# Memory tokens requested earlier, diagonal staging shared by two engines, and the loads and staging of a prologue reordered

## What is computed

```python
def reference(x, mem, ...):
    for i in range(2):
        if i == 0:
            proj = rmsnorm(x, e_norm) @ e_w_in
            out_a = gmlp_spatial_gate(gelu(a_u), gelu(a_v), e_gmlp_w, e_gmlp_b)
            out_b = silu(layernorm(causal_depthwise_conv31(a * sigmoid(g), e_conv_w)))
            mix = concatenate([out_a, out_b]) @ e_w_out
        else:
            u = rmsnorm(x, o_norm) @ o_w_in
            y = s5_layer(u, lam, log_dt, b, c, d)      # state 64 per group, 32 groups
            mix = glu(gelu(y) @ o_w_out)
        x = x + mix
        memn = rmsnorm(mem, ca_mem_norm[i])
        x = x + attention(rmsnorm(x), k=memn @ ca_wk[i], v=memn @ ca_wv[i])
        x = x + swiglu(rmsnorm(x))
    return rmsnorm(x)
```

## Time and profile before

| | us |
|---|---|
| median of 2 runs | 5374.97 |
| the two runs | 5334.44 and 5415.51 |
| the profiled execution | 5339.59 |
| span of its slowest core (core 4) | 5338.0 |
| spans of its other cores | 5275.0 to 5325.3 |

### The profile page before, as it was taken

How to read it: one execution, slowest core, us unless ns; L and a number is a source line. 1 busy time by engine, 2 the same in 40 slices (tenths; PEclk the granted TensorE clock), 3 DMA queues, 4 the chain that set the end, 5 groups by cost and what they waited for, 6 DMA issues and landing times.

```text
span 5338.0 us, 96207 instructions; the slowest of 8 cores (5275.0 to 5338.0 us)
## 1 busy us (share of the span) xinstructions
PE 4340.5 (81%) x35399; PEld 3515.4 (66%) x35449; DVE 2148.8 (40%) x4562; ACT 1462.6 (27%) x3458; POOL 298.4 (6%) x320
## 2 busy tenths in 40 slices
PE   0332897989979897888979897988979898888978
PEld 0221587767857687766857586766858577666867
DVE  2354523434343533435342433435252433435252
ACT  0122412243132422233132422233131421333131
POOL 0000000000000000000000000000000000000000
PEclk9866997989889997999889897998889997999889
DMA  4115587765678587665768576665868576675866
GB/s 73 40 58 136 95 137 174 105 134 90 167 127 140 95 139 174 93 133 89 176 125 137 100 114 194 90 138 93 181 120 126 116 108 191 91 141 89 176 120 107
DMA packets 457748, 657.94 MB, mean 123 GB/s; under 512 B 19553, under 2 KB 368433, under 8 KB 446800
## 3 DMA queue, kind: packets, MB, share of 16 engines
q0 software_dynamic: 410560, 427.84, 53.6%
q1 hardware_dynamic: 38480, 223.66, 11.9%
q10 hardware_dynamic: 8256, 0.29, 0.1%
HBM read 1041.95 MB, written 37.62 MB: 202 GB/s over the span
## 4 chain that ended last, share of the span: by engine, by line
PE 67%; DMA 14%; DVE 9%; issue 6%; ACT 4%; ACTq 0%; DVEq 0%; POOL 0%; POOLq 0%; SPq 0%
PE ps L183 65%; DMA ring<-ffn_w_down 5%; DMA ring<-o_w_out 3%; DVE s5t L200 3%; DVE aux L215 3%; PE ps L187 2%; DMA xT<-o_c_re 1%; ACT L197 1%; DMA ring<-ffn_w_gate 1%; DMA xT<-o_c_im 1%; ACT bigbf L197 1%; DVE bigbf L200 1%; DMA ring<-e_w_in 1%; DMA ring<-ffn_w_up 0%; ACT sq L197 0%
## 5 line engine op out<-in xcount | busy, mean ns | idle before, releaser
L183 PE MATMUL ps<-xn,ring 128*128 128x256 bf16 x15488 | 1886.1, 284 | 60.2 <-DVE hbuf L200 31.5
L183 PEld LDWEIGHTS ps<-xn,ring 128*128 128x128 bf16 x15488 | 1562.1, 101 | 380.0 <-issue 147.1
L183 PE MATMUL ps<-bigbf,ring 128*128 128x256 bf16 (+1 forms) x13824 | 1480.5, 278 | 221.8 <-DMA ring<-o_w_out 102.1
L183 PEld LDWEIGHTS ps<-bigbf,ring 128*128 128x128 bf16 x13824 | 1336.1, 109 | 362.4 <-issue 237.4
L197 ACT ACTIVATE scr<-ps 128x256 f32<-128x256 f32 (+1 forms) x992 | 398.5, 405 | 1432.5 <-PE ps L183 1079.0
L200 DVE TENSOR_TENSOR bigbf<-scr,ps 128x256 bf16<-128x256 f32 x704 | 295.7, 421 | 890.1 <-PE ps L183 889.9
L200 DVE TENSOR_TENSOR xT<-xT,ps 128x256 f32<-128x256 f32 x640 | 258.9, 420 | 657.2 <-PE ps L183 639.6
L197 ACT ACT_TABLE_LOAD x204 | 261.7, 1283 | 682.3 <-PE ps L183 349.1
L197 ACT ACTIVATE sq<-xT 128x256 bf16<-128x256 f32 x768 | 259.1, 406 | 370.2 <-DVE xT L200 369.1
L209 DVE SCALAR_TENSOR_TENSOR xn<-xT,gv,rstd 128x256 bf16<-128x256 f32 x768 | 312.5, 479 | 10.4 <-DVE rstd L215 0.5
L197 ACT ACTIVATE bigbf<-ps 128x256 bf16<-128x256 f32 (+1 forms) x544 | 211.3, 396 | 375.1 <-PE ps L183 352.3
(11 more groups left out here) (147 smaller groups left out, 2300.2 us busy)
## 6 DMA issues: line engine op xcount, KB each, us to landing
ring<-scr_s SPq DMA_DIRECT2D x64, 2048.0 KB, 8.5
ring<-ffn_w_gate POOLq DMA_DIRECT2D x80, 1024.0 KB, 10.2
ring<-ffn_w_up POOLq DMA_DIRECT2D x80, 1024.0 KB, 9.1
ring<-ffn_w_down POOLq DMA_DIRECT2D x32, 2112.0 KB, 20.4
ring<-e_w_in POOLq DMA_DIRECT2D x16, 2048.0 KB, 15.9
ring<-ca_wq POOLq DMA_DIRECT2D x16, 2048.0 KB, 19.3
ring<-ca_wo POOLq DMA_DIRECT2D x16, 2048.0 KB, 21.8
ring<-scr_diag SPq DMA_DIRECT2D x16, 1984.0 KB
```

What stands on the lines that cost most here:

```text
L183: self.S.op("pe", lambda h: h.matmul(out, lhsT, rhs, start=start, stop=stop), reads=R, writes=W)
```

## The change

Three edits, all in the prologue.

1. The load of the memory tokens and the first three weight loads of `pro_mem` become a function `pro_mem_loads`, called right after the gains' transpose. `pro_mem` takes the weights from a list.
2. `pro_gmlp_conv` is called right after that, ahead of `pro_s5_loads` and of the loads of `fg` and `bsbc`. Its two temporary tiles lie in `s5t` instead of `bigf`, which now holds the memory tokens.
3. In the staging, every second diagonal is made by ScalarE (an Identity activation with the tap's column as scale) instead of VectorE, with a buffer of its own for the ordering; the DMA of each half waits for both engines.

```diff
--- before.py
+++ after.py
@@ -354,14 +354,17 @@
         pb, bpb = self.bank()
         self.tr(pb[:, 0:128], G, bG, [bpb])
         self.cp(gv[:, 0:G_N], pb[:, 0:G_N], [bpb], cW)
+        need_mem = "ca0" in self.phases or "ca1" in self.phases
+        if need_mem:
+            self.pro_mem_loads()
+        if "l0mix" in self.phases:
+            self.pro_gmlp_conv()
         if "l1mix" in self.phases:
             self.pro_s5_loads()
         self.dma("sp", self.fg[:], p["final_norm"].partition_broadcast(128), [], cW)
         self.dma("sp", self.bsbc[:].rearrange("p g i -> p (g i)"),
                  p["e_gmlp_b"][0].rearrange("g i -> (g i)").partition_broadcast(128), [], cW)
-        if "l0mix" in self.phases:
-            self.pro_gmlp_conv()
-        if "ca0" in self.phases or "ca1" in self.phases:
+        if need_mem:
             self.pro_mem()
         if "l1mix" in self.phases:
             self.pro_s5()
@@ -369,29 +372,33 @@
     def pro_gmlp_conv(self):
         p = self.p
         cW = [self.b_const]
-        wtmp = self.bigf[:, 0, :].rearrange("p (g j) -> p g j", g=4)
-        self.dma("sp", wtmp, p["e_gmlp_w"][0].rearrange("g i j -> i g j"), [], [self.b_bf[0]])
+        wtmp = self.s5t[:, 0, 0:512].rearrange("p (g j) -> p g j", g=4)
+        self.dma("sp", wtmp, p["e_gmlp_w"][0].rearrange("g i j -> i g j"), [], [self.b_s5t[0]])
         for g in range(4):
             pb, bpb = self.bank()
-            self.tr(pb[:, 0:128], wtmp[:, g, :], [self.b_bf[0]], [bpb])
+            self.tr(pb[:, 0:128], wtmp[:, g, :], [self.b_s5t[0]], [bpb])
             self.cp(self.gw[:, g, :], pb[:, 0:128], [bpb], cW)
             self.memset(self.gw[64:128, g, 0:64], 0.0, cW)
-        cw = self.bigf[:, 1, :]
-        self.memset(cw, 0.0, [self.b_bf[1]])
-        self.dma("sp", cw[0:31, :], p["e_conv_w"][0], [], [self.b_bf[1]])
+        cw = self.s5t[:, 1, 0:512]
+        self.memset(cw, 0.0, [self.b_s5t[1]])
+        self.dma("sp", cw[0:31, :], p["e_conv_w"][0], [], [self.b_s5t[1]])
         cwT = self.aux[:, 0, 0:128].rearrange("p (f k) -> p f k", k=32)
         for fc in range(4):
             pb, bpb = self.bank()
-            self.tr(pb[:, 0:128], cw[:, fc * 128:(fc + 1) * 128], [self.b_bf[1]], [bpb])
+            self.tr(pb[:, 0:128], cw[:, fc * 128:(fc + 1) * 128], [self.b_s5t[1]], [bpb])
             self.cp(cwT[:, fc, 0:31], pb[:, 0:31], [bpb], [self.b_aux[0]])
         stage = self.bigbf[:].rearrange("p a b -> p (a b)")
         for half in range(2):
             for i in range(62):
                 fc = half * 2 + i // 31
                 k = i % 31
-                self.ts(stage[:, i * 128:(i + 1) * 128], self.ident[:], cwT[:, fc, k:k + 1], None, ALU.mult, None,
-                        [self.b_aux[0], self.b_const], [self.b_bb[0]])
-            self.dma("sp", self.diag_d[half], stage[:, 0:62 * 128], [self.b_bb[0]], [self.b_diag])
+                if i % 2 == 0:
+                    self.ts(stage[:, i * 128:(i + 1) * 128], self.ident[:], cwT[:, fc, k:k + 1], None, ALU.mult, None,
+                            [self.b_aux[0], self.b_const], [self.b_bb[0]])
+                else:
+                    self.act(stage[:, i * 128:(i + 1) * 128], self.ident[:], AF.Identity, [self.b_aux[0], self.b_const],
+                             [self.b_bb[1]], scale=cwT[:, fc, k:k + 1])
+            self.dma("sp", self.diag_d[half], stage[:, 0:62 * 128], [self.b_bb[0], self.b_bb[1]], [self.b_diag])
 
     def rms_generic(self, src_fn, bsrc, n, gcol, dst_fn, bdst, rstd=None, brstd=None, sqbufs=None):
         if rstd is None:
@@ -414,10 +421,16 @@
             self.stt(dst_fn(dc), src_fn(dc), self.gv[:, gcol + dc:gcol + dc + 1], rstd,
                      ALU.mult, ALU.mult, [bsrc[dc], brstd, self.b_const], [bdst[dc]])
 
+    def pro_mem_loads(self):
+        p = self.p
+        memtok = self.bigf[:, 0:4, :].rearrange("p a b -> p (a b)").rearrange("p (m d) -> p m d", m=2)
+        self.dma("sp", memtok, self.mem_d.rearrange("(m p) d -> p m d", p=128), [], self.b_bf[0:4])
+        self.mem_w = [self.load_w(p["ca_wk"][0], 0, 1024), self.load_w(p["ca_wv"][0], 0, 1024),
+                      self.load_w(p["ca_wk"][1], 0, 1024)]
+
     def pro_mem(self):
         p = self.p
         memtok = self.bigf[:, 0:4, :].rearrange("p a b -> p (a b)").rearrange("p (m d) -> p m d", m=2)
-        self.dma("sp", memtok, self.mem_d.rearrange("(m p) d -> p m d", p=128), [], self.b_bf[0:4])
         memT = self.bigf[:, 4:8, :].rearrange("p a b -> p (a b)").rearrange("p (c m) -> p c m", c=8)
         bmT = [self.b_bf[4 + dc // 2] for dc in range(8)]
         for dc in range(8):
@@ -428,14 +441,14 @@
         for li in range(2):
             self.rms_generic(lambda dc: memT[:, dc, :], bmT, 256, G_MEM + 8 * li,
                              lambda dc: self.xn[:, dc, 0:256], self.b_xn)
-            wk, bwk = self.load_w(p["ca_wk"][li], 0, 1024)
+            wk, bwk = self.mem_w[2 * li]
             for oc in range(8):
                 pb, bpb = self.bank()
                 for dc in range(8):
                     self.mm(pb[:, 0:256], wk[:, dc, oc * 128:(oc + 1) * 128], self.xn[:, dc, 0:256], dc == 0, dc == 7,
                             [bwk, self.b_xn[dc]], [bpb])
                 self.act(self.KT[:, li, oc, :], pb[:, 0:256], AF.Copy, [bpb], [self.b_KT])
-            wv, bwv = self.load_w(p["ca_wv"][li], 0, 1024)
+            wv, bwv = self.mem_w[1] if li == 0 else self.load_w(p["ca_wv"][li], 0, 1024)
             for mc in range(2):
                 for half in range(2):
                     pb, bpb = self.bank()
```

## The result

| | before | after |
|---|---|---|
| ratio of the runs compared | 1 | 1.0113 (95% interval 1.0096 to 1.013) |
| profiled execution, us | 5339.6 | 5390.5 |
| span of its slowest core, us | 5338.0 (core 4) | 5388.9 (core 1) |
| start of the loop, mean of 8 cores, us | 485.0 | 539.3 |
| length of the loop, mean of 8 cores, us | 4819.9 | 4821.0 |

The change makes the kernel 1.1% slower. 5339.6 x 1.0113 is 5400 us, the forecast total. The median of the 11 runs after is 5401.5 us; that of the 10 runs before is 5528 us, because in some executions the cores of a die are slowed whatever the kernel, in seven of these ten, and among them the 5415.5 us that went into the 5375 us shown ahead of the prediction; the ratio is made without them, from runs of 5334.4 to 5341.3 us before and 5385.9 to 5404.6 us after.

A forecast was written before the change was run, and what follows sets the result against it. It took 64 small transfers on ScalarE's queue to end the prologue. Staging end 106.4, loads 8, 27.2 and 1, transfers 90, company 3 give squares at 236 us, 60 later: 5400 us in total, range 5362 to 5462.

The forecast's parts named there:

- What bounds the prologue: Prologue: 64 small transfers on ScalarE's queue set its end; tokens and staging are ready 23 us before ScalarE is.
- Part 1 and 2: Prologue: earlier calls of the weight loads and an earlier request of the memory tokens gain 0 us each.
- Part 3, the staging: Staging of the diagonals: starts at 73 us, ends at 106.4 instead of 141, 35 us earlier but worth 0.
- the startup is relieved: Rival, 11%: with 4-byte packets gone from the startup, gains chain faster and staging starts 19 us sooner; +41, 5381 us.
- Part 4, what the reordering moves: ScalarE's stream: small and xT loads wait behind the staging until 106.4 us, so squares start at 236, 60 us later.
- the sum of the small loads: Behind the staging: o_lam loads 8 us together, two o_log_dt 27.2, first xT landing 1 us later; bounds 16 to 67.
- The 63 transfers: Rest of the xT loads on ScalarE's queue: 1.43 us each, 90 us together, bounds 86 and 110.
- The sum against the shown median: Whole kernel: 5400 us is 0.5% more than the shown median of 5375, 1.1% more than the profiled execution.
- Cheap small loads: Rival, 20%: behind the staging the four small loads land in 4.1 us each, 16 and not 35; +41 us, 5380.
- dear ones: Rival, 8%: o_lam_im keeps its 35.3 us and the diagonals' write delays the rest, 31 us on top; 5431 us.
- a change that counts as intended: Rival, 1%: the change does what it says and counts, which needs tokens or staging to be last in the prologue.
- The loop's rhythm: Rival, 5%: in the loop, the later start gives core 4 the pace of core 1, 53 us less, 5347 us.

The follow-up runs named there:

- e6: The kernel before, with a buffer of its own for each of the 64 loads to xT, so none waits for the one before; fastest run 5314.5 us.
- e7: The changed kernel, with the three early weight loads called in pro_mem again; one run, 5398.8 us.
- e2: The changed kernel, with the call of the S5 loads moved back and the staging on VectorE alone; ratio 1.0002 against the kernel before.
- e1: The changed kernel, with the call of the S5 loads moved back and the staging still split; ratio 1.0076 against the kernel before.
- e3: The changed kernel, with the staging on VectorE alone and the S5 loads' call left behind it; ratio 1.0118 against the kernel before.
- e4: The changed kernel, with only the four small loads issued ahead of memory loads and staging again; ratio 1.0103 against the kernel before.
- e8: The changed kernel, with the 64 transfers first and unchained, small loads unchained behind the staging, fg and bsbc in own buffers; fastest run 5284.6 us.
- e9: The kernel of e8, with the four small loads issued by SyncE instead of ScalarE; ratio 0.9916 against the kernel before.

## Why the prediction was right, and where it was not

**What bounds the prologue: right.** That the 64 small transfers on ScalarE's queue, and neither the tokens nor the staging, set the end of the prologue is shown by e6: unchaining them alone starts the loop 15 us sooner, and on cores 2 to 5 the squares 22 us sooner, close to the 23 of the prediction.

**Part 1 and 2: right.** The weights moved by nothing (e7), the early tokens were worth about 1 us (e2).

**Part 3, the staging: the end right to 4 us, by errors that cancel.** It started at 63.5 us, not 73. The rival "the startup is relieved" was real, at under a third of its 19 us: the last gain was issued 5.5 us sooner. And `e_gmlp_w`, which I had given 9 us, 4 of them behind the tokens, took 5.3: it landed beside the tokens (50.7 us against 49.8), with no `o_log_dt` ahead of it. But a half took 16.9 and 15.3 us on ScalarE, not 14 and 12.7. The term that was mis-sized is the 0.30 us for the 128 x 128 form, which I placed between the 254 and 403 ns of rows 6: it takes 403 ns, as long as 128 x 256, and 0.49 us from one to the next.

**Part 4, what the reordering moves: right in mechanism; the sum of the small loads right by luck.** From the end of the staging to the landing of the first transfer I had 39 us (8 + 27.2 + 1, and 3 for company); on core 1 it took 36 (102.3 to 138.5). Its terms were off both ways: `o_lam_re` and `o_lam_im` took 13.4 and 13.7 us to land, not 4.1 each, but the next issues did not wait for these landings, so they cost the 1.5 us of their issues and not 8; the two `o_log_dt` took 22.7 and 11.6 us (17.2 is their median), 34 and not 27.2. The 63 transfers, 90 us forecast, took 93 (138.5 to 231.4), 1.47 us each. The 2.0 us of the Trainium skill's page ("DMA: Bandwidth & Descriptors", section "Anatomy of one DMA — SWDGE (gpsimd) path") would have given, as an estimate, 126; the page gives that figure for DMAs that GpSimd issues, these were ScalarE's. Squares: forecast 236 us, measured 231.8 on core 1.

**What the part left out.** It reads as if the moved call and the activations added up. e1 and e3 show that each alone loses most or all of it (40 us at the squares on cores 2 and 3 of e1, 64 in the mean of e3): with the split alone the staging waits for the transfers, with the move alone the transfers wait for the memset behind the staging. Only both undone give the time back.

**The sum against the shown median: wrong.** The delay of 60 us and the total of 5400 us held (54 us at the loop's start; 1.13% of 5339.6 is 60). The step that failed is the base of "against the median of the two runs shown, 5375, this is 0.5% more". The term that was mis-sized is the 5375: the runs of before that were compared took 5334.4 to 5341.3 us, and the 5415.5 us in that median is none of them. So the change is 1.13%, more than twice the 0.5% and the other figure of that sentence. The prediction had seen that the median lay 35 us above the profiled execution and still named it as the base. Two runs 81 us apart were no base to name a change of 25 us against; the profiled execution was.

**The rivals.** Cheap small loads (16 us), dear ones (67 us) and a change that counts as intended all fell: on core 1 the small loads and the first transfer cost 36. The loop's rhythm fell as well: the loop's mean length is 4819.9 us before and 4821.0 after. Of the relieved startup the saving came, but not the way: on core 1 of after six gains in a row still come 5.7 us apart (4.09 to 38.54 us), as before, and only the last ones are quick (43.28, 44.63), since the weights end sooner: the slowest of their three loads took 40.2 us to land, against 48.2 on core 4 of before. That a gain waits less because fewer queues take turns, as I drew from the Trainium skill's page "DMA: Bandwidth & Descriptors", section "Queues, rings and completion order", these rows do not show.

## What to carry to other kernels

Before a DMA issue is moved on a compute engine's stream, list everything in front of it and behind it there: an in-order engine that issues loads is held by their waits, and its loads are held by its instructions. Ask first which stream is last; making two early things earlier cost 54 us here because a third, late one went behind them. And look at why a run of small transfers is slow: one dependency too coarse (a buffer for eight disjoint writes) was worth 62 us in the changed kernel, more than the change cost, and 15 us in the kernel before.

## What the runs showed of the hardware

- **A load of 4-byte pieces holds other queues' loads.** With the second `o_log_dt` (4 KB) issued ahead of it on ScalarE's queue, `e_gmlp_w` (256 KB) on SyncE's took 12.4 to 23.1 us to land on 21 cores of e1 to e4; issued ahead of it or within 0.1 us, 6.1 to 9.9 on the other 11; in after, without it, 5.3 to 6.6.
- **It can hold its issuing engine too, without a semaphore.** The first issue of `o_log_dt`, behind 16 KB of such pieces, lasted 11.6 us on core 1 of e8 and 11.8 us on core 1 of after (8.9 to 13.5 and 7.4 to 11.8 over the cores), and on core 1 it ended within 0.4 us of the landing of `o_lam_re`; the second issue took 0.6 us in both. With these loads on SyncE's queue the squares started 15 us sooner (e9 against e8). What holds the issue was not looked for.
- **In each pair of cores one is slower.** Before, cores 0, 2, 4 and 6 take 4836 to 4854 us for the loop and cores 1, 3, 5 and 7 take 4793 to 4804; after, the slower ones are 1, 3, 4 and 6. In e1 to e7 and e9 each pair (0 and 1, 2 and 3, and so on) has one of each too, 27 to 53 us apart, and which one it is changes. After, cores 0 to 3:

```profile
core 0: 5340.0 us, clock 0.889
core 1: 5388.9 us, clock 0.886
core 2: 5335.3 us, clock 0.886
core 3: 5374.8 us, clock 0.877
```

The cause was not looked for. The slowest core sets the time, so the difference is about as large as what the change cost.
